# A hybrid attention layer: the FoX part of the merge is added by GpSimd instead of VectorE

## What is computed

```python
z = rmsnorm(x) @ w_in            # q, k, v of both branches, forget logits, gates g_fox, g_swa
o_fox = forgetting_attention(...)         # 8 heads
o_swa = sliding_window_attention(...)     # 8 query heads, 2 key heads
y = sigmoid(g_fox) * (o_fox @ w_proj_fox) + sigmoid(g_swa) * (o_swa @ w_proj_swa)
x = x + rmsnorm(y @ w_o)
u, v = split(rmsnorm(x) @ w_up)
x = x + rmsnorm((gelu(causal_conv3(u) + b) * v) @ w_down)
```

## Time and profile before

| | us |
|---|---|
| runs without profile | 1667.5, 1666.9, 1660.91 (median 1666.9) |
| the profiled execution, its own time | 1663.6 |
| its span in the trace | 1661.8 |
| TensorE busy | 1585.9 |
| VectorE busy | 971.0 |
| GpSimd busy | 559.7 |
| ScalarE busy | 439.7 |
| granted TensorE clock, mean | 0.991 |

### The profile page before, as it was taken

The page is one execution under the profiler, slowest core; times in us unless marked ns, Lnnn a source line. Parts: engine busy times, 40 slices in busy tenths (PEclk is TensorE's granted clock), DMA queues, the critical chain, the costliest instruction groups (busy, mean ns, idle before and its releaser), DMA issues.

```text
span 1661.8 us, 24389 instructions
## 1 busy us (share of the span) xinstructions
PE 1585.9 (95%) x9375; PEld 1482.6 (89%) x9375; DVE 971.0 (58%) x1830; ACT 439.7 (26%) x910; POOL 559.7 (34%) x304
## 2 busy tenths in 40 slices
PE   5999999999999898988999999999999999999996
PEld 5999999999989888877888999899998999989995
DVE  6776657767753388864545654454544545445456
ACT  4143534344332255644222101010010101101013
POOL 6242322222223322242332325343353433534343
PEclk9999999999999999999999999999999999999998
DMA  6442222122135401166320111111111111111115
GB/s 192 65 119 69 71 67 69 48 69 60 35 124 167 156 26 52 52 194 206 115 92 29 51 39 51 44 45 50 38 50 40 48 50 38 50 38 50 50 38 106
DMA packets 129614, 122.88 MB, mean 74 GB/s; under 512 B 7453, under 2 KB 116377, under 8 KB 129537
## 3 DMA queue, kind: packets, MB, share of 16 engines
q1 hardware_dynamic: 93513, 66.38, 13.7%
q10 hardware_dynamic: 34824, 51.13, 9.8%
q0 software_dynamic: 1200, 4.33, 1.5%
HBM read 94.00 MB, written 27.92 MB: 73 GB/s over the span
## 4 chain that ended last, share of the span: by engine, by line
PE 85%; DVE 9%; DMA 2%; issue 1%; ACT 1%; ACTq 0%; SPq 0%; POOL 0%; POOLq 0%; DVEq 0%
PE bank L703 18%; PE bank L704 17%; PE bank L705 17%; PE bank L709 7%; PE bank L711 7%; PE bank L710 7%; PE bank L735 4%; PE bank L826 2%; DMA gm<-d_mfox 1%; PE bank L797 1%; PE bank L796 1%; DVE m_l L2006 1%; DVE rowsn L1636 1%; DVE p L1875 1%; PE bank L1063 1%
## 5 line engine op out<-in xcount | busy, mean ns | idle before, releaser
L599 POOL TENSOR_TENSOR ring_h<-raw,att 128x1024 fp32r<-128x1024 f32 x108 | 210.0, 1944 | 927.9 <-PE bank L705 752.6
L703 PE MATMUL bank<-m_h,ring_h 128*128 128x352 f32 x1056 | 340.7, 323 | 0.7 <-DVE m_l L1541 0.7
L704 PE MATMUL bank<-m_l,ring_h 128*128 128x352 f32 x1056 | 338.6, 321 | 0.0
L705 PE MATMUL bank<-m_h,ring_l 128*128 128x352 f32 x1056 | 338.4, 320 | 0.0
L600 POOL TENSOR_TENSOR ring_l<-raw,ring_h 128x1024 fp32r<-128x1024 f32 x108 | 288.4, 2670 | 8.5
L703 PE MATMUL bank<-ht_h,ring_h 128*128 128x352 f32 x840 | 279.2, 332 | 0.2 <-DVE vqn L1552 0.2
L705 PE MATMUL bank<-ht_h,ring_l 128*128 128x352 f32 x840 | 273.4, 325 | 0.0
L704 PE MATMUL bank<-ht_l,ring_h 128*128 128x352 f32 x840 | 272.8, 325 | 0.0
L703 PEld LDWEIGHTS bank<-m_h,ring_h 128*128 128x128 f32 x1056 | 198.1, 188 | 1.2 <-DVE m_l L1541 0.8
L704 PEld LDWEIGHTS bank<-m_l,ring_h 128*128 128x128 f32 x1056 | 198.4, 188 | 0.4
L705 PEld LDWEIGHTS bank<-m_h,ring_l 128*128 128x128 f32 x1056 | 198.0, 188 | 0.0
(11 more groups left out here) (275 smaller groups left out, 2595.7 us busy)
## 6 DMA issues: line engine op xcount, KB each, us to landing
raw<-in_w_up SPq DMA_DIRECT2D x44, 512.0 KB, 3.9
raw<-in_w_in SPq DMA_DIRECT2D x35, 512.0 KB, 3.9
raw<-in_w_down SPq DMA_DIRECT2D x22, 512.0 KB, 3.6
d_gate<-gst ACTq DMA_DIRECT2D x48, 176.0 KB, 1.9
gm<-d_gate ACTq DMA_DIRECT2D x8, 528.0 KB, 4.3
d_mfox<-mst ACTq DMA_DIRECT2D x8, 528.0 KB, 3.0
gm<-d_gate ACTq DMA_DIRECT2D x24, 176.0 KB, 2.9
gm<-d_mfox ACTq DMA_DIRECT2D x24, 176.0 KB, 3.5
```

The lines of the kernel that those rows point to most:

```text
L599: order.link(nc.gpsimd.tensor_tensor(high, src, zero.to_broadcast(list(src.shape)), ALU.add))
L703: nc.tensor.matmul(out, wh, xh, start=start, stop=False)
L704: nc.tensor.matmul(out, wh, xl, start=False, stop=False)
L705: return nc.tensor.matmul(out, wl, xh, start=False, stop=stop)
```

## The change

GpSimd adds the FoX part, in its own program, in groups placed in front of the low parts of w_o; m32 gets a third slot; VectorE no longer adds, and makes the low part of chunk i-2 behind the product of chunk i.

```diff
-    m32, _ = place("m32", [P, 2, CH], offset=R3 + 8 * KT * TOK)
+    m32, o2 = place("m32", [P, 3, CH], offset=R3 + 8 * KT * TOK)
+    assert o2 + 12 * CH <= nc.sbuf_usable_end
@@ GpSimd
+            def merge_adds(items):
+                for i in items:
+                    pool.wait_ge(freed_dve, reads["dve"][first_chunk[S_WS] + i + 1])
+                    pool.wait_ge(gm2_in[i % 3], 32 * (i // 3 + 1))
+                    nc.gpsimd.tensor_tensor(m32[:, i % 3, :], m32[:, i % 3, :], gm2[:, i % 3, 1, :], ALU.add
+                                            ).then_inc(m_sum, 1)
+            ADDS = [2, 4, 6, 10, 13, 16, 19, 24]
             for n in range(S_FFN):
+                name, k = SLABS[n]
+                if name == "wo":
+                    merge_adds(range(ADDS[k - 1] if k else 0, ADDS[k]))
                 pool.wait_ge(raw_in[n % NRAW], 16 * (n // NRAW + 1))
-                name, k = SLABS[n]
@@ ScalarE
-                copy(m_h[:, j, CH * c:CH * c + CH], m32[:, i % 2, :]).then_inc(mh_done, 1)
+                copy(m_h[:, j, CH * c:CH * c + CH], m32[:, i % 3, :]).then_inc(mh_done, 1)
@@ VectorE, merge_low
-                V.tensor_tensor(m_l[:, j, sl], m32[:, i % 2, :], m_h[:, j, sl].bitcast(F32), ALU.subtract
+                V.tensor_tensor(m_l[:, j, sl], m32[:, i % 3, :], m_h[:, j, sl].bitcast(F32), ALU.subtract
@@ VectorE, the loop over the chunks
-                wait(dve, m_ready, M_FOX + i - 1 if i >= 2 else 0)
-                V.tensor_tensor(m32[:, i % 2, :], bank[q % 3][:, 0:CH], gm2[:, i % 3, 0, :], ALU.mult
+                wait(dve, m_ready, M_FOX + i - 2 if i >= 3 else 0)
+                V.tensor_tensor(m32[:, i % 3, :], bank[q % 3][:, 0:CH], gm2[:, i % 3, 0, :], ALU.mult
                                 ).then_inc(freed_dve, 1)
-                if i >= 1:
-                    merge_low(i - 1)
-                dve.wait_ge(freed_dve, reads["dve"][q + 1])
-                V.tensor_tensor(m32[:, i % 2, :], m32[:, i % 2, :], gm2[:, i % 3, 1, :], ALU.add
-                                ).then_inc(m_sum, 1)
+                if i >= 2:
+                    merge_low(i - 2)
+            merge_low(3 * KT - 2)
             merge_low(3 * KT - 1)
```

## The result

The changed kernel took 1671.41 us (median of 9 runs, 1667.83 to 1674.53) against 1665.68 us before (9 runs): ratio 1.0034, 95% interval 1.0023 to 1.0045, so some 5.7 us slower. The profiled execution took 1672.83 us, with a span of 1671.0.

A forecast was written before the change was run, and what follows sets the result against it. The prediction took the merge to be bound by a three-chunk ring through sum, copy, load, sigmoid and product. Its terms, 0.8 + 3.15 + 1.6 + 1.8 = 7.35, taken as 7 us, gave 1673.9 us by the median, range 1665 to 1681.

The forecast's parts named there:

- the forecast case of +5 to +9: Whole kernel: the main forecast, 5 to 9 us slower than before, chance 0.50.
- the ring through the loads: Merge: sum, ScalarE's copy, load, sigmoid and product three chunks on set the pace, 6.7 us a round; TensorE does not.
- The price of a sum: GpSimd in the merge: one 128x352 addition taken as 0.9 us, against 0.52 us on VectorE.
- Term 1: Merge rounds before the split of the last projection slab: two rounds 0.4 us longer each, 0.8 us.
- Term 2: Split of the last projection slab on GpSimd: sum 6 waits behind it, 3.95 us later, 3.15 us added.
- Term 3: Merge rounds after the split, chunks 10, 13, 16 and 19: four times 0.4 us, 1.6 us.
- Term 4: Merge end: first w_o matmul waits for chunk 21's low part behind product 23; 2.2 less 0.4 slack, 1.8 us.
- w_o part 7 would not be last: Merge end: the path through sum 23 and w_o part 7 moves by only 5.5 + 0.4 us and does not decide.
- The sum: Whole kernel: the forecast delays add to 7.35 us, taken as 7 us.
- (a): Merge: the rounds absorb the delay through emptier DMA and earlier products; -2 to +4 us, chance 0.20.
- (b): Merge: costlier hand-overs between GpSimd and VectorE, 1.4 us a sum and late w_o parts; +9 to +14 us, chance 0.24.
- (c): Merge: VectorE's queue sets the pace, so removing its sums returns TensorE's 8.0 us of waits; down to 1659 us, chance 0.06.

The follow-up runs named there:

- Experiment 8: Gate load given its own semaphore and issued earlier: in the changed kernel 1662.64 us; on top of experiment 7, sums on VectorE, 1658.52 us.
- experiment 7: The kernel before, with VectorE's sum directly behind its product and the low part after it: 1664.04 us, ratio 0.9990.
- experiment 2: The changed kernel with the low part of chunk i-2 ahead of product i: 1672.99 us, ratio 1.0048 to the kernel before.
- experiment 6: The changed kernel with only the low part of chunk 21 moved ahead of product 23: 1670.05 us, ratio 1.0033 to the kernel before.
- the repeated ones: Both kernels profiled again unedited: merge 64.45 and 59.76 us for the kernel before, 66.35 us for the changed kernel.
- experiment 1: The changed kernel with sum 6 ahead of the last projection slab's split and sum 7 between its halves: 1668.01 us, ratio 1.0013 to before.
- Experiment 3: The changed kernel with a second GpSimd addition, of zero, before each of the 24 sums: 1678.15 us, ratio 1.0078 to the kernel before.
- experiment 4: The changed kernel's third buffer and low part two chunks behind, but sums kept on VectorE: 1666.69 us, ratio 1.0007 to the kernel before.

## Why the prediction was right

Forecast were 7 us more and 0.42% against the median; measured were 5.7 us and 0.34%, inside the forecast case of +5 to +9 and on its lower side.

- **What bounds the merge.** Right: the ring through the loads, not TensorE and not VectorE. Experiment 8 shows it by taking the sigmoid off the FoX load and sending the gate earlier: 7.1 us of merge in the changed kernel, 4.9 us from experiment 7 to 8 with the sums on VectorE.
- **The price of a sum.** 0.9 was taken, 0.94 us is what it takes undisturbed and 1.14 to 1.24 behind a low part of VectorE (1.15 on average over all 24). That the low part starts first and GpSimd waits for it was forecast. The Trainium skill, page SBUF — State Buffer, section Who interferes with whom, has the rule: a VectorE instruction with two inputs in SBUF contends with a GpSimd one that reads SBUF, for a port pair that is an exclusive lock, and the order of issue decides who blocks. The rows agree in both directions: VectorE's low part took 2.49 us behind a GpSimd instruction (experiment 2), GpSimd's sum 1.14 us behind a low part (experiment 6).
- **Term 1**, 0.8 us before the split: 0.73 measured at copy 4 between the first two profiles; with the repeated ones it is 0.45 to 1.47.
- **Term 2**, sum 6 later by 3.95 us: 3.83, and 26.8 to 27.6 us in the profiles of the change against 23.0 to 23.3 in those of before. As a cost in the end it was forecast at 3.15 us; experiment 1 gets 2.2 of it back.
- **Term 3**, "Chunks 10, 13, 16 and 19: four times 0.4, 1.6 us", is the step that failed. From copy 6 to copy 19 the change needs 31.01 and 31.21 us, the kernel before 31.07 and 30.51 (34.23 with the late load). The sum took the increment from product to sum for the increment of the whole round, whereas most of a round is loads that differ from one to the next by more than 0.4 us, and GpSimd was still idle for 0.84 to 1.51 us in each. Experiment 3 shows the other side of that edge, where 0.9 us more per sum adds some 2 us a round. What exactly took up the 0.4 us in each round, loads or slack of ScalarE, stays open.
- **Term 4**, 1.8 us at the end. The order of the low parts costs 1.2 to 1.3 us (last column of the table; experiment 4 without GpSimd), not 2.2, as product 23 follows product 22 after 1.09 us here. Taking the order away alone gave nothing back, since sum 22 then holds the same low part (experiment 6). The wait of 0.4 us for w_o part 7 did go away, but the first half tile was no shorter for it (8.12 us against 7.69). The later load 22, 1.3 us in these two profiles, was in no term, whether it is chance or not. That w_o part 7 would not be last held: no matmul of the change waits for it.
- **The sum.** 7.35 us were added up and the merge is 6.2 us longer. The 1.6 us of term 3 that did not come were largely replaced by the 1.3 us of load 22 that no term held. To that extent it is luck that the sum comes so near; terms 1 and 2 came as reasoned, and term 4 with two thirds of its size.
- **Rivals.** (a) had term 3 right and terms 2 and 4 wrong. (b) did not come about, but experiment 3 shows that one more instruction per chunk on GpSimd brings it (1678.15 us). (c) fell: taking the sums off VectorE returned nothing (TensorE waits 8.8 us for products instead of 8.0), and what did make the kernel faster was parting the loads.

## What to carry to other kernels

Where one buffer ring sets the pace, ask of each wait in it whether the waiting instruction needs all that its semaphore counts: parting two loads that shared one semaphore was worth 0.35 to 0.5% here, as much as the choice of engine for the sum or more. Moving work to an engine that also does long instructions in a fixed order costs little until its work fills the round, and then nearly all that is added; count the round's work there before, and look for the longest block in front of a short, urgent instruction. And where VectorE and GpSimd both read two operands from SBUF, put the instruction that does not touch the other engine (here the product from PSUM) ahead of the one that may be held; the opposite order gained nothing in experiment 2. Last, when an edit moves an instruction behind a later one, as the low part of chunk 21 behind product 23, look at what the later one waits for: it cost 1.2 us in the change and stood in a wait of 4.3 us once the rounds had become faster.

## What the runs showed that was not expected

TensorE's granted clock. In windows of the trace (columns: PE, PEld, DVE, ACT, POOL busy, then the granted clock, DMA share, GB/s), the changed kernel:

```profile
746.00:756.00 10.00, 9.91 (x50) 9.06 (x50) 5.65 (x8) 5.69 (x10) 7.15 (x6) 0.83 0.64 190
756.00:766.00 10.00, 8.04 (x41) 7.78 (x40) 4.23 (x8) 5.26 (x11) 8.38 (x7) 0.83 0.71 230
```

and the kernel before at the same distance:

```profile
744.00:754.00 10.00, 7.54 (x45) 6.76 (x44) 6.77 (x13) 5.12 (x11) 4.24 (x2) 1.00 0.61 192
```

After the idle of 4.39 us that term 2 opened (until 745.12 us), and again after one of 1.96 us (until 759.13), the granted clock fell in parts of these stretches from 2.4 to 1.2 GHz; in this profile of before, with idle times of at most 2.38 us there, it did not. It is not the change's alone: in the second profile of before TensorE was idle for 2.47 us until 760.21, and the clock of the stretch from 760 to 764 us is 0.59. At the lower level the chunk's matmuls start 0.29 us apart instead of 0.16. The changed kernel's chain of waits runs through TensorE from 759.13 to 768.60 us, and product 18 waited 1.05 us for it, so in that round TensorE was the bound after all; the shift did not grow by it. The first half tile with w_o took 8.12 us after an idle of 5.38 in the change and 7.69 after 2.88 before, but the repeated profiles give 7.42 for the change and 8.41 and 7.44 for before, so this difference is not shown to be the change's.

The other surprise was the spread of equal loads: FoX loads of 176 KB landed after 2.4 to 6.1 us within one execution, and the late one of chunk 15 lengthened its round by 2.9 us, half of what the whole change costs.
